# Sparse attention in a two-block transformer kernel: compressed keys stored ahead of the first key set and scored with it, their softmax done per head, retained values transposed one unit sooner

## The chip, the cores and the metric

The kernel runs on one core of one Trainium2 chip. The metric is the device time of one execution in microseconds (us); less is better. The core's engines each run their own instruction stream and meet at semaphores: TensorE (PE, with PEld for its weight loads), VectorE (DVE), ScalarE (ACT), GpSimd (POOL) and SyncE (SP, which only issues the weight DMAs here).

## The reference, cut to what matters

Two transformer blocks on 512 tokens of width 1024. The change lies in the second block, in its sparse attention (`_nsa`), with 16 heads of width 64 in 2 key groups:

```
s_c = einsum('bghqd,bgnd->bghqn', qc, kc) * scale          # 31 compressed keys (windows of 32 tokens)
p_c = _masked_softmax(s_c, cmp_end[None, :] <= t[:, None])
o_c = einsum('bghqn,bgnd->bghqd', p_c, vc)
...                                                        # selected blocks: here all 8 blocks of 64 tokens are taken
o_s = softmax(q . k_slc, causal) . v_slc
o_w = softmax(q . k_win, causal) . v_win
return gc[..., 0:1] * o_c + gc[..., 1:2] * o_s + gc[..., 2:3] * o_w
```

With 512 tokens the selection takes every block and the window covers every key, so each head has two causal attentions over 512 keys (`m` = 0 selected, `m` = 1 window) and a third over the 31 compressed keys, padded to 32. Beside it the block has a retention branch, whose values `rv` are projected, centred and transposed in the same stretch of the program.

## The kernel before

**Units and steps.** `sparse_attention` runs 32 units U. Four of them make a group i = U // 4, which is a pair of heads; the place u = U % 4 in it is called a step here, and stands for (head j, key set m) = (0,0), (0,1), (1,0), (1,1). Each engine has a part that loops over the 32 units in a fixed, hand-written order; semaphores with absolute counts order the parts against each other.

**What TensorE does in a step** (`pe_part`): it transposes the probabilities of U by key blocks kb (`turn(U, 0)`, `turn(U, 1)`: 7 transposes, `bank<-ident,nprob`), does the first half of a projection of 1024 x 128 weights (`fill`, 12 matmuls of 512 columns, three for each of 4 tiles, since every product is made of high and low parts), transposes the rest (`turn(U, 2)`, `turn(U, 3)`: 3 transposes), does the second half of `fill` (12 matmuls), then scores unit U + 2 (`score`, 4 query blocks qb of (qb + 1) x 128 keys, each with two matmuls), and last multiplies by the values (`values`, 8 matmuls). The transposes kb = 2 and 3 go into the banks of kb = 0 and 1, and so wait until VectorE has read those (`lo`).

**What is done for the compressed keys**, once in a group: `compressed_scores(i + 1)` in step 2, 16 matmuls of 32 columns for both heads, into bank 7; `compressed_shift(i + 1)` on VectorE at the start of step 3 (mask, row maximum, subtraction: 3 instructions of 256 elements); `compressed_exps` on ScalarE in step 3; `compressed_scale(i)` on VectorE in step 0; then `compressed_turn(i, 0)` at the end of step 0 and `compressed_turn(i, 1)` in step 1 (4 transposes each, `bank<-ident,cpad`), each copied out of bank 7 as a high part by ScalarE (`cpt_hi`) and a low part by VectorE (`cpt_lo`), and used by `compressed_values` (`bank<-cpt_hi,vcs`) in steps 0 and 2. `retained_values(i)` (`bank<-centre,rv_t`) uses the same bank 7 in step 2.

**What VectorE does in a step**, in order (`dve_part`): `biased(U + 1)`, which adds the mask to the scores of the next unit and takes the row maxima (L2382, four, with a small instruction behind, L2387); the low parts of the transposes kb = 0 and 1 (`npt_lo`, L2422); extra work of the step; the low parts kb = 2 and 3; `scaled(U + 1)` (three small instructions and four of L2405); and the low part of a weight chunk (`w_lo`, L162). ScalarE in a step makes the high parts (`npt_hi`, L2280), the exponentials (L2251) and the high part of the weight chunk.

**Where a score goes.** Query blocks are scored in the order 0, 2, 1, 3: blocks 0 and 2 in bank 0, block 1 in bank 1, block 3 in bank 2. `score` of a unit waits for the `biased` of the unit before it on the same banks.

Of the kernel before, what the change touches and what calls it, by code (L numbers as in the profile page):

```python
# [79 lines left out]
def build_program(nc, stream, xt, cols, tables, rows, decays, pos, w2, out):  # L80
    top = ExitStack()
    with top:
# [1552 lines left out]
        kc_a = sb("kc_a", [P, 32], F32R, A0 + 11 * K)  # L1635
        kc_b = sb("kc_b", [P, 32], F32R, A0 + 11 * K + 256)
# [18 lines left out]
        nk_a = sb("nk_a", [P, 2, S], F32R, A0 + 64 * K)  # L1655
        nk_b = sb("nk_b", [P, 2, S], F32R, A0 + 68 * K)
        nvs = sb("nvs", [P, TB, 2, P], F32R, A0 + 72 * K)
# [369 lines left out]
        def sparse_attention(start):  # L2027
# [6 lines left out]
                                              "c_scored", "c_dve", "c_exp", "c_turned", "c_hi", "c_lo", "zero",  # L2034
# [20 lines left out]

            def score(pe, U):
                j, m = units[U % 4]
                if U % 16 < 2:
                    pe.wait_ge(s["k_lo"], k_ready(U // 16, m))
                if U % 4 == 0:  # L2060
                    pe.wait_ge(s["q_done"], 2 * (U // 4 + 1))
                for n, qb in enumerate(SCORE_ORDER):
                    at_least(pe, s["biased"], 4 * (U - 1) + max(n, 1) + 1, z["biased"])
                    at = slice(qb * P, (qb + 1) * P)
                    mm2(score_bank(qb), nq[:, j, at], nk_a[:, m, 0:(qb + 1) * P], nk_b[:, m, 0:(qb + 1) * P]
                        ).then_inc(s["scored"], 1)

            def compressed_bank(i):
                return banks[7] if i else banks[3]

            def compressed_scores(pe, i):
                pe.wait_ge(s["q_done"], 2 * i + 2)
                pe.wait_ge(s["k_lo"], k_ready(i // 4, "kc"))
                at_least(pe, s["rv_lo"], i)
                for j in range(2):
                    for qb in range(TB):
                        at = slice(qb * P, (qb + 1) * P)
                        last = mm2(compressed_bank(i)[:, (TB * j + qb) * 32:(TB * j + qb + 1) * 32], nq[:, j, at],
                                   kc_a[:], kc_b[:])
                    last.then_inc(s["c_scored"], 1)  # L2080

            def first_scores(pe):
                pe.wait_ge(q["out"], 12)
                compressed_scores(pe, 0)
                score(pe, 0)

            def pe_part(pe):
# [54 lines left out]
                for U in range(UNITS):  # L2142
# [8 lines left out]
                    if U == 0:  # L2151
                        pe.wait_ge(s["c_dve"], 1)
# [20 lines left out]
            def high_k(g):  # L2173
                for m in range(2):
                    k = nqk[:, g + 8 + 2 * m, :]
                    nc.scalar.activation(nk_a[lower, m, :], k[lower], ACT.Copy).then_inc(s["k_hi"], 1)
                    nc.scalar.activation(nk_b[upper, m, :], k[upper], ACT.Copy).then_inc(s["k_hi"], 1)
# [36 lines left out]
            def low_k(pool, g, base):  # L2214
                for m in range(2):
                    k = nqk[:, g + 8 + 2 * m, :]
                    for n, (r, to, hi) in enumerate(((lower, nk_b, nk_a), (upper, nk_a, nk_b))):
                        pool.wait_ge(s["k_hi"], base + 2 * m + n + 1)
                        nc.gpsimd.tensor_tensor(to[r, m, :], k[r], hi[r, m, :], ALU.subtract).then_inc(s["k_lo"], 1)
# [22 lines left out]
            def compressed_exps(act, i):  # L2242
                act.wait_ge(s["c_dve"], 10 * i + 3)
                nc.scalar.activation(csc[:], csc[:], ACT.Exp, scale=0.125).then_inc(s["c_exp"], 1)
# [9 lines left out]
            def first_exps(act):  # L2254
                exps(act, 0, range(TB))
                compressed_exps(act, 0)

            def act_part(act):

                def stage_k(g):  # L2260
                    at_least(act, s["scored"], 64 * g, z["scored"])
                    at_least(act, s["c_scored"], 8 * g)
# [51 lines left out]
                for U in range(UNITS):  # L2314
# [8 lines left out]
                    if u == 1:  # L2323
                        compressed_high(i, 1)
                    if u == 2:
# [8 lines left out]
                    if u == 0:  # L2334
                        compressed_high(i, 0)
                    ahead(high_part, act, fn, U)
                    if u == 1 and i < 7:
                        stage_q(i + 1)
                        if i == 3:
                            stage_k(1)  # L2340
                    if u == 3 and i < 7:
                        compressed_exps(act, i + 1)
# [13 lines left out]
            add = cmp_add[:].rearrange("p (o t) n -> p o t n", o=1).to_broadcast([P, 2, TB, 32])  # L2356
            keep = cmp_keep[:].rearrange("p (o t) n -> p o t n", o=1).to_broadcast([P, 2, TB, 32])
            over = [t.rearrange("p (h t o) -> p h t o", h=2, o=1).to_broadcast([P, 2, TB, 32])
                    for t in (c_top, c_inverse)]

            def step(dve, i, instruction, count, wait=True):

                instruction.then_inc(s["c_dve"], 1)
                if wait:
                    dve.wait_ge(s["c_dve"], 10 * i + count)

            def compressed_shift(dve, i):
                dve.wait_ge(s["c_scored"], 2 * i + 2)
                step(dve, i, nc.vector.tensor_tensor(
                    csc[:], compressed_bank(i)[:, 0:256].rearrange("p (h t n) -> p h t n", h=2, t=TB), add, ALU.add), 1)  # L2370
                step(dve, i, nc.vector.tensor_reduce(c_top.rearrange("p (h t) -> p h t", h=2), csc[:], AX.X, ALU.max), 2)
                step(dve, i, nc.vector.tensor_tensor(csc[:], csc[:], over[0], ALU.subtract), 3, False)

            def biased(dve, U):
                for place_of, qb in enumerate(SCORE_ORDER):
# [6 lines left out]
                    nc.vector.tensor_tensor_reduce(nprob[:, U % 2, scores_rows(qb)], score_bank(qb),  # L2382
# [24 lines left out]
            def first_shift(dve):  # L2407
                compressed_shift(dve, 0)
# [6 lines left out]
            def dve_part(dve):  # L2415
# [26 lines left out]
                def compressed_scale(i):  # L2442
                    dve.wait_ge(s["c_exp"], i + 1)
                    step(dve, i, nc.vector.tensor_tensor(csc[:], csc[:], keep, ALU.mult), 4)
                    step(dve, i, nc.vector.tensor_reduce(c_total.rearrange("p (h t) -> p h t", h=2), csc[:], AX.X, ALU.add), 5)
                    step(dve, i, nc.vector.tensor_scalar(c_total, c_total, 1e-20, None, ALU.max), 6)
                    step(dve, i, nc.vector.reciprocal(c_total, c_total), 7)
                    step(dve, i, nc.vector.tensor_tensor(
                        c_inverse.rearrange("p (h t) -> p h t", h=2), c_total.rearrange("p (h t) -> p h t", h=2),
                        gates[:, :, i * 6:i * 6 + 6].rearrange("p t (h c) -> p h t c", c=3)[:, :, :, 0], ALU.mult), 8)  # L2450
                    for j in range(2):

                        diagonal = cpad[:, j, :].rearrange("p (t w) -> p t w", w=P + 32)[:, :, 0:32]
                        step(dve, i, nc.vector.tensor_tensor(diagonal, csc[:, j, :, :], over[1][:, j, :, :], ALU.mult), 9 + j,
                             False)
# [9 lines left out]
                for U in range(UNITS):  # L2465
                    i, u = U // 4, U % 4
                    if u == 3 and i < 7:
                        compressed_shift(dve, i + 1)
# [3 lines left out]
                    if u == 0:  # L2472
                        compressed_scale(i)
                        if i:
                            joined(i - 1, 1)
                    if u == 1:
                        compressed_low(i, 1)
                    if u == 2:
                        retained_low(i)
                    lows(U, (2, 3))  # L2480
                    if u == 0:
                        compressed_low(i, 0)
                    if u == 2:
                        joined(i, 0)
# [604 lines left out]
```

## Time and profile before

| | |
|---|---|
| median of 3 runs | 2149.85 us (2149.74 to 2151.31) |
| the profiled execution | 2148.9 us, of which the traced span is 2147.2 us |
| PE busy | 2107.7 us (98%) |
| DVE busy | 1328.0 us (62%) |
| ACT busy | 1006.7 us (47%) |
| POOL busy | 690.0 us (32%) |
| mean granted TensorE clock | 0.993 |
| stretch of the 32 units | about 1229 to 1556 us from the span's start |

Times in the trace are microseconds from the start of the span; L2382 is line 2382 of the kernel. A timeline row of TensorE shows its start and a modelled end, so a matmul's price in a dense stream is read from the start of one row to the start of the next. In a row of VectorE or ScalarE the second figure is the instruction's length, or with `xN` behind it that of N in a row.

### The profile page before, as it was taken

The page shows a single profiled execution, that of the slowest core. Times are in us where ns is not written, and L with a number is a line of the kernel's source. Part 1 is how long each engine was busy: PE and PEld are TensorE (multiplying, and loading weights), DVE is VectorE, ACT ScalarE, POOL GpSimd, SP SyncE. Part 2 cuts the span into 40 slices and gives each one's busy share as a digit, 9 for nine tenths or more (in the row PEclk, how much of TensorE's full clock was granted, in tenths as well). Part 3 has the DMA queues.
Part 4 walks back from the last instruction along what each step waited for, and adds up shares of the span by engine and source line. Part 5 has one row for each costly group of instructions (what it writes and reads, how often), then busy time and mean ns, then how long its engine had stood idle before and what let it go on. Part 6 is the DMA issues. An engine that isn't in the chain of part 4 may idle for free.

```text
span 2147.2 us, 31300 instructions
## 1 busy us (share of the span) xinstructions
PE 2107.7 (98%) x10824; PEld 1784.2 (83%) x10824; DVE 1328.0 (62%) x2185; ACT 1006.7 (47%) x1770; POOL 690.0 (32%) x515
## 2 busy tenths in 40 slices
PE   8999999999999999999999999999999999999997
PEld 6887888889988888898887788888877888889886
DVE  5467774467672276765268788788768336676524
ACT  4345564533442263344234467676656325334322
POOL 2011345323233262443325601211165415132331
PEclk9999999999999999999999999999999999999999
DMA  5212235243433333443334322222264533434331
GB/s 171 79 50 69 84 121 183 94 134 140 163 115 108 95 117 117 147 161 103 98 102 147 118 69 70 84 74 77 86 210 140 185 98 118 136 131 166 105 95 62
DMA packets 73423, 248.15 MB, mean 116 GB/s; under 512 B 8080, under 2 KB 8336, under 8 KB 72944
## 3 DMA queue, kind: packets, MB, share of 16 engines
q1 hardware_dynamic: 51120, 182.08, 26.8%
q0 software_dynamic: 10496, 37.56, 5.1%
q10 hardware_dynamic: 11712, 27.27, 3.5%
q8 instruction: 57, 0.93, 0.2%
q14 instruction: 38, 0.31, 0.1%
HBM read 227.48 MB, written 18.87 MB: 115 GB/s over the span
## 4 chain that ended last, share of the span: by engine, by line
PE 85%; DVE 8%; ACT 2%; issue 2%; POOL 2%; DMA 1%; DVEq 0%; SPq 0%; ACTq 0%; POOLq 0%
PE bank L188 25%; PE bank L189 24%; PE bank L190 24%; PE bank L194 3%; PE bank L195 3%; POOL hid L709 2%; PE bank L2095 2%; DVE w_lo L162 1%; DVE gn_r L2697 1%; DVE xn_lo L587 1%; PE bank L883 1%; PE bank L2756 1%; PE bank L2758 1%; DMA w_raw<-stream 1%; DVE blk L1929 1%
## 5 line engine op out<-in xcount | busy, mean ns | idle before, releaser
L162 DVE TENSOR_TENSOR w_lo<-w_raw,w_hi 128x1024 fp32r<-128x1024 f32 x337 | 449.9, 1339 | 424.7 <-ACT w_hi L157 422.1
L188 PE MATMUL bank<-xn_hi,w_hi 128*128 128x512 f32 (+1 forms) x1432 | 555.0, 388 | 7.0 <-DVE w_lo L162 6.1
L157 ACT ACTIVATE w_hi<-w_raw 128x1024 fp32r<-128x1024 f32 x337 | 354.6, 1054 | 409.5 <-PE bank L190 248.2
L189 PE MATMUL bank<-xn_lo,w_hi 128*128 128x512 f32 (+1 forms) x1432 | 540.6, 378 | 0.0
L190 PE MATMUL bank<-xn_hi,w_lo 128*128 128x512 f32 (+1 forms) x1432 | 540.0, 377 | 0.0
L188 PEld LDWEIGHTS bank<-xn_hi,w_hi 128*128 128x128 f32 x1432 | 271.7, 190 | 58.3 <-DVE w_lo L162 7.2
L190 PEld LDWEIGHTS bank<-xn_hi,w_lo 128*128 128x128 f32 x1432 | 270.7, 189 | 50.2
L189 PEld LDWEIGHTS bank<-xn_lo,w_hi 128*128 128x128 f32 x1432 | 271.6, 190 | 45.4 <-issue 2.6
L188 PE MATMUL bank<-down_hi,w_hi 128*128 128x512 f32 x528 | 205.9, 390 | 0.0
L190 PE MATMUL bank<-down_hi,w_lo 128*128 128x512 f32 x528 | 205.6, 389 | 0.0
L189 PE MATMUL bank<-down_lo,w_hi 128*128 128x512 f32 x528 | 205.6, 389 | 0.0
L763 POOL TENSOR_TENSOR down_lo<-h,down_hi 128x512 fp32r<-128x512 f32 x66 | 111.9, 1700 | 252.9 <-ACT down_hi L543 252.9
L189 PEld LDWEIGHTS bank<-down_lo,w_hi 128*128 128x128 f32 x528 | 99.1, 188 | 20.9 <-issue 0.2
L188 PEld LDWEIGHTS bank<-down_hi,w_hi 128*128 128x128 f32 x528 | 99.2, 188 | 20.6 <-POOL down_lo L763 0.2
L190 PEld LDWEIGHTS bank<-down_hi,w_lo 128*128 128x128 f32 x528 | 99.1, 188 | 20.6
L509 ACT ACTIVATE snaps<-bank 128x256 f32<-128x256 f32 x96 | 36.8, 384 | 164.9 <-PE bank L190 164.8
L498 ACT ACTIVATE silu<-silu 128x512 f32<-128x512 f32 x66 | 41.6, 631 | 150.9 <-DVE silu L596 85.7
L714 POOL DMA_DIRECT2D s_raw<-stream x48 | 26.5, 553 | 231.7 <-DVE s_lo L609 231.2
L2211 POOL TENSOR_TENSOR q_low<-nqk,nq 64x512 f32<-64x512 f32 x16 | 21.4, 1336 | 213.2 <-ACT nq L2195 212.5
L601 DVE TENSOR_TENSOR h<-silu,h 128x512 f32 (+1 forms) x66 | 84.3, 1277 | 4.4
L190 PE MATMUL bank<-t_hi,s_lo 128*128 128x256 f32 x288 | 81.6, 283 | 0.0
L189 PE MATMUL bank<-t_lo,s_hi 128*128 128x256 f32 x288 | 81.5, 283 | 0.0
(451 smaller groups left out, 4261.8 us busy)
## 6 DMA issues: line engine op xcount, KB each, us to landing
w_raw<-stream SPq DMA_DIRECT2D x337, 512.0 KB, 3.6
s_raw<-stream POOLq DMA_DIRECT2D x48, 512.0 KB, 6.3
spill_g<-gate_out ACTq DMA_DIRECT2D x16, 256.0 KB, 2.0
m_more<-spill_g POOLq DMA_DIRECT2D x3, 1024.0 KB, 12.8
x<-xt SPq DMA_DIRECT2D x4, 512.0 KB, 7.7
x<-xt ACTq DMA_DIRECT2D x1, 2048.0 KB, 9.9
spill_x<-x ACTq DMA_DIRECT2D x1, 2048.0 KB, 6.4
spill_ga<-ga_out ACTq DMA_DIRECT2D x8, 256.0 KB, 2.0
```

Source lines behind the costliest of these rows:

```text
L157: nc.scalar.activation(w_hi[:, slot, :], w_raw[:, slot % 2, :], ACT.Copy).then_inc(split_hi, 1)
L162: nc.vector.tensor_tensor(w_lo[:, slot, :], w_raw[:, slot % 2, :], w_hi[:, slot, :], ALU.subtract).then_inc(split_lo, 1)
L188: nc.tensor.matmul(to, a_hi, b_hi, start=start, stop=False, skip_group_check=True)
L189: nc.tensor.matmul(to, a_hi, b_lo, start=False, stop=False, skip_group_check=True)
L190: return nc.tensor.matmul(to, a_lo, b_hi, start=False, stop=stop, skip_group_check=True)
L194: nc.tensor.matmul(to, both, first, start=start, stop=False, skip_group_check=True)
L195: return nc.tensor.matmul(to, both, second, start=False, stop=stop, skip_group_check=True)
L498: nc.scalar.activation(silu[t][:], silu[t][:], ACT.Silu).then_inc(s["silu"], 1)
L601: nc.vector.tensor_tensor(to, silu[t][:], to, ALU.mult).then_inc(s["product"], 1)
L709: nc.gpsimd.tensor_tensor(total_sq, squares[:, 0, :] if k == 1 else total_sq, squares[:, k % 4, :], ALU.add).then_inc(m["added"], 1)
L763: nc.gpsimd.tensor_tensor(down_lo[:, j % 4, :], h[:, bass.ds(k * S, S)], down_hi[:, j % 4, :], ALU.subtract).then_inc(s["lo"], 1)
L2095: last = nc.tensor.transpose(banks[4 + kb % 2][:, (qb - kb) * P:(qb - kb + 1) * P], nprob[:, U % 2, OFF[qb] + kb * P:OFF[qb] + (kb + 1) * ...
```

## The change

What it does:

- The high and low compressed keys `kc_a`, `kc_b` become the first 32 columns of `nk_a`, `nk_b`, directly in front of key set m = 0.
- `compressed_scores` is gone. In a `score` with m = 0, the matmuls of query blocks 0, 1 and 2 take 32 columns more (160, 288, 416 in place of 128, 256, 384), and block 3, which fills a bank by itself, gets a separate pair of 32 columns, written into bank 1. The query blocks are scored in the order 0, 1, 2, 3 (0 and 1 in bank 0, 2 in bank 1, 3 in bank 2).
- The softmax of the compressed keys is done per head: `compressed_shift(i, 1)` at the start of VectorE's step 1 and `compressed_shift(i + 1, 0)` at the start of its step 3, each 5 instructions; `compressed_exps` in steps 1 and 3; `compressed_scale(i, 0)` in step 0 and `compressed_scale(i, 1)` in step 2, each 6 instructions on 128 elements or fewer.
- `compressed_turn(i, 1)` moves from step 1 to the end of step 2 (its `cpt_hi` and `cpt_lo` with it), and `retained_values(i)` from step 2 to step 1 (with `rv_hi_out` and `rv_lo_out`).

```diff
-        kc_a = sb("kc_a", [P, 32], F32R, A0 + 11 * K)
-        kc_b = sb("kc_b", [P, 32], F32R, A0 + 11 * K + 256)
...
-        nk_a = sb("nk_a", [P, 2, S], F32R, A0 + 64 * K)
-        nk_b = sb("nk_b", [P, 2, S], F32R, A0 + 68 * K)
+        nk_a = sb("nk_a", [P, NC + 2 * S], F32R, A0 + 64 * K)
+        nk_b = sb("nk_b", [P, NC + 2 * S], F32R, A0 + 68 * K + 4 * NC)
+        kc_a, kc_b = nk_a[:, 0:NC], nk_b[:, 0:NC]
...
+            NORDER = range(TB)
+            AT_C = (banks[0][:, 0:NC], banks[0][:, NC + P:2 * NC + P], banks[1][:, 0:NC], banks[1][:, NC + 3 * P:2 * NC + 3 * P])
...
-                for n, qb in enumerate(SCORE_ORDER):
+                for n, qb in enumerate(NORDER):
                     at_least(pe, s["biased"], 4 * (U - 1) + max(n, 1) + 1, z["biased"])
...
+                    if m == 0 and qb < TB - 1:
+                        last = mm2(rows_with_windows(qb), nq[:, j, at], nk_a[:, 0:NC + width], nk_b[:, 0:NC + width])
+                    else:
+                        last = mm2(rows_bank(qb), nq[:, j, at], keys(nk_a, m, width=width), keys(nk_b, m, width=width))
+                    if m == 0 and qb == TB - 2:
+                        last = mm2(AT_C[TB - 1], nq[:, j, (TB - 1) * P:S], kc_a, kc_b)
+                    last.then_inc(s["scored"], 1)
...
                 def compressed_turn(i, j):
-                    if j == 0:
-                        pe.wait_ge(s["c_dve"], 10 * i + 10)
+                    pe.wait_ge(s["c_dve"], 11 * (2 * i + j + 1))
+                    at_least(pe, s["rv_lo"], i + j)
...
                 def retained_values(i):
                     pe.wait_ge(s["cleared"], 4 * i + 1)
-                    pe.wait_ge(s["c_lo"], 2 * i + 2)
+                    pe.wait_ge(s["c_lo"], 2 * i + 1)
...
                     if u == 1:
-                        compressed_turn(i, 1)
-                    if u == 2:
                         retained_values(i)
...
-                    if u == 0:
-                        compressed_turn(i, 0)
-                    if u == 2 and i < 7:
-                        compressed_scores(pe, i + 1)
+                    if u % 2 == 0:
+                        compressed_turn(i, u // 2)
...
+            def compressed_shift(dve, i, j):
+                dve.wait_ge(s["scored"], 4 * (4 * i + 2 * j) + 3 + z["scored"])
+                near = banks[0][:, 0:2 * (NC + P)].rearrange("p (t w) -> p t w", w=NC + P)[:, :, 0:NC]
+                step(dve, i, j, nc.vector.tensor_tensor(csc[:, j, 0:2], near, cmp_add[:, 0:2], ALU.add), 1, False)
+                for qb in (2, 3):
+                    step(dve, i, j, nc.vector.tensor_tensor(csc[:, j, qb], AT_C[qb], cmp_add[:, qb], ALU.add), qb, qb == 3)
+                step(dve, i, j, nc.vector.tensor_reduce(of_head(c_top, j), csc[:, j], AX.X, ALU.max), 4)
+                step(dve, i, j, nc.vector.tensor_tensor(csc[:, j], csc[:, j], over_windows(c_top, j), ALU.subtract), 5, False)
...
                 for U in range(UNITS):
                     i, u = U // 4, U % 4
+                    if u == 1:
+                        compressed_shift(dve, i, 1)
                     if u == 3 and i < 7:
-                        compressed_shift(dve, i + 1)
+                        compressed_shift(dve, i + 1, 0)
                     if U + 1 < UNITS:
                         biased(dve, U + 1)
                     lows(U, (0, 1))
```

**The order on VectorE, from the end of step 0 into step 1** (L162 is the last instruction of step 0; the ISA rows are `biased`, `npt_lo` the low parts that `turn(U, 2)` and `turn(U, 3)` wait for). Before:

```order
L162 TENSOR_TENSOR w_lo<-w_raw,w_hi 128x1024
L2382 ISA nprob,small<-bank,bias_tri 128x128
L2382 ISA small 128x1
L2382 ISA nprob,small<-bank,bias_tri 128x384
L2382 ISA small 128x1
L2382 ISA nprob,small<-bank,bias_tri 128x256
L2382 ISA small 128x1
L2382 ISA nprob,small<-bank,bias_tri 128x512
L2382 ISA small 128x1
L2387 TENSOR_SCALAR small<-small 128x4
L2422 TENSOR_TENSOR npt_lo<-bank,npt_hi 128x512
L2422 TENSOR_TENSOR npt_lo<-bank,npt_hi 128x384
```

The same place of the changed kernel, up to the first instructions of `biased`:

```order
L162 TENSOR_TENSOR w_lo<-w_raw,w_hi 128x1024
L2367 TENSOR_TENSOR csc<-bank,cmp_add 128x64
L2369 TENSOR_TENSOR csc<-bank,cmp_add 128x32 x2
L2370 TENSOR_REDUCE small<-csc 128x4
L2371 TENSOR_TENSOR csc<-csc,small 128x128
L2381 ISA nprob,small<-bank,bias_tri 128x128
L2381 ISA small 128x1
L2381 ISA nprob,small<-bank,bias_tri 128x256
```

Five instructions now stand between the weight chunk and `biased`; the rest of `biased`, its small instruction and the two `npt_lo` follow as before. Between steps 2 and 3 the same five stand, where three on 256 elements stood.

**The order on TensorE at the end of step 2** (the first row is the last matmul of `fill`; `kc`, 16 matmuls in all, are `compressed_scores`; `nk` is `score`; `cpt` is `compressed_values`). Before, with 13 more `kc` rows in the gap:

```order
L190 MATMUL bank<-xn_hi,w_lo 128x512
L194 MATMUL bank<-kc_a,nq 128x32
L195 MATMUL bank<-kc_b,nq 128x32
...
L195 MATMUL bank<-kc_b,nq 128x32
L194 MATMUL bank<-nk_a,nq 128x128
L195 MATMUL bank<-nk_b,nq 128x128
L194 MATMUL bank<-nk_a,nq 128x384
L195 MATMUL bank<-nk_b,nq 128x384
```

The same place of the changed kernel:

```order
L190 MATMUL bank<-xn_hi,w_lo 128x512
L2114 MATMUL bank<-ident,cpad 128x128 x4
L194 MATMUL bank<-nk_a,nq 128x160
L195 MATMUL bank<-nk_b,nq 128x160
L194 MATMUL bank<-nk_a,nq 128x288
L195 MATMUL bank<-nk_b,nq 128x288
L194 MATMUL bank<-nk_a,nq 128x416
L195 MATMUL bank<-nk_b,nq 128x416
L194 MATMUL bank<-nk_a,nq 128x32
L195 MATMUL bank<-nk_b,nq 128x32
L194 MATMUL bank<-nk_a,nq 128x512
L195 MATMUL bank<-nk_b,nq 128x512
```

The 16 narrow matmuls are gone, and the four transposes of `cpad` have come in their place; behind the scores `cpt` follows as before, now with its input made just in front of it. The end of step 0 reads the same as this in the changed kernel.

## Rows read from the trace of the kernel before

**Rows 1.** The page: the span, and the engines' busy time.

```profile
span 2147.2 us, 31300 instructions
PE 2107.7 (98%) x10824; PEld 1784.2 (83%) x10824; DVE 1328.0 (62%) x2185; ACT 1006.7 (47%) x1770; POOL 690.0 (32%) x515
```

**Rows 2.** Busy time by stretch, a group's length; start:end, length, then engines.

```profile
1312.00:1353.00 41.00, 40.87 (x236) 35.46 (x236) 32.80 (x100) 28.31 (x67) 5.15 (x4) 1.00 0.25 78
```

**Rows 3.** Timeline, TensorE, step 2 to the next step 2; start, us.

```profile
1298.71 0.18 PE L194 MATMUL bank<-kc_a,nq 128*128 128x32 f32 x1
...
1300.41 0.31 PE L194 MATMUL bank<-nk_a,nq 128*128 128x128 f32 x1
...
1307.25 0.48 PE L188 MATMUL bank<-xn_hi,w_hi 128*128 128x512 f32 x1
...
1310.48 0.34 PE L195 MATMUL bank<-nk_b,nq 128*128 128x384 f32 x1
1310.66 0.28 PE L194 MATMUL bank<-nk_a,nq 128*128 128x256 f32 x1
1310.78 0.28 PE L195 MATMUL bank<-nk_b,nq 128*128 128x256 f32 x1
...
1319.21 0.60 PE L2111 MATMUL bank<-ident,cpad 128*128 128x128 f32 x4
...
1321.22 0.50 PE L194 MATMUL bank<-cpt_hi,vcs 128*128 128x512 f32 x1
...
1327.22 0.48 PE L188 MATMUL bank<-xn_hi,w_hi 128*128 128x512 f32 x1
...
1340.07 0.18 PE L194 MATMUL bank<-kc_a,nq 128*128 128x32 f32 x1
```

**Rows 4.** Timeline, VectorE, the same stretch: steps 3, 0 and 1.

```profile
1301.72 0.42 DVE L2369 TENSOR_TENSOR csc<-bank,cmp_add 128x256 f32<-128x256 f32 x1
1302.17 0.42 DVE L2371 TENSOR_REDUCE small<-csc 128x8 f32<-128x256 f32 x1
1302.63 0.42 DVE L2372 TENSOR_TENSOR csc<-csc,small 128x256 f32<-128x256 f32 x1
1302.97 0.28 DVE L2382 CUSTOM_DVE_ANT_0 nprob<-bank,bias_tri 128x128 f32<-128x128 f32 x1
...
1304.81 1.15 DVE L2422 TENSOR_TENSOR npt_lo<-bank,npt_hi 128x512 fp32r<-128x512 f32 x2
...
1320.48 0.69 DVE L2434 TENSOR_TENSOR cpt_lo<-bank,cpt_hi 128x512 fp32r<-128x512 f32 x1 [1.82 <-ACT cpt_hi L2286]
...
1325.86 1.15 DVE L2422 TENSOR_TENSOR npt_lo<-bank,npt_hi 128x512 fp32r<-128x512 f32 x2
```

**Rows 5.** Groups by line and shape, VectorE, 1292.14 to 1333.5; mean ns.

```profile
L2422 DVE TENSOR_TENSOR npt_lo<-bank,npt_hi 128x128 fp32r<-128x128 f32 x4 | 1.1, 281 | 0.0
```

**Rows 6.** Timelines, TensorE and VectorE, into the first unit.

```profile
1217.38 0.25 PE L194 MATMUL bank<-kc_a,nq 128*128 128x32 f32 x1
...
1233.10 0.79 PE L2095 MATMUL bank<-ident,nprob 128*128 128x128 f32 x3 [0.92 <-DVE npt_lo L2422]
...
1219.34 0.42 DVE L2369 TENSOR_TENSOR csc<-bank,cmp_add 128x256 f32<-128x256 f32 x1 [0.90 <-PE bank L195]
...
1220.90 0.28 DVE L2382 CUSTOM_DVE_ANT_0 nprob<-bank,bias_tri 128x128 f32<-128x128 f32 x1
```

**Rows 7.** Timeline, TensorE, group 3 (new keys are staged); its first and last row.

```profile
1360.57 0.60 PE L2111 MATMUL bank<-ident,cpad 128*128 128x128 f32 x4
...
1382.95 0.28 PE L194 MATMUL bank<-kc_a,nq 128*128 128x32 f32 x1 [0.71 <-ACT nq L2202]
...
1405.14 0.60 PE L2111 MATMUL bank<-ident,cpad 128*128 128x128 f32 x4
```

**Rows 8.** Busy time by stretch, TensorE alone, group 3; then its granted clock.

```profile
1384.70:1388.15 3.45, 3.45 (x12) 0.51 0.63 233
```

**Rows 9.** Timeline, TensorE, unit 30, where its second `fill` half ends.

```profile
1550.07 0.39 PE L194 MATMUL bank<-cpt_hi,vcs 128*128 128x512 f32 x1
```

More of the change, by code:

```diff
@@ L2061, in score @@
                     pe.wait_ge(s["q_done"], 2 * (U // 4 + 1))
-                for n, qb in enumerate(SCORE_ORDER):
+                for n, qb in enumerate(NORDER):
                     at_least(pe, s["biased"], 4 * (U - 1) + max(n, 1) + 1, z["biased"])
[L2064 to L2080, printed above, removed]
+                    at, width = slice(qb * P, (qb + 1) * P), (qb + 1) * P
+                    if m == 0 and qb < TB - 1:
[5 more added lines that the diff above has]
+                    last.then_inc(s["scored"], 1)
             def first_scores(pe):
                 pe.wait_ge(q["out"], 12)
-                compressed_scores(pe, 0)
                 score(pe, 0)
@@ L2218, in low_k @@
                         pool.wait_ge(s["k_hi"], base + 2 * m + n + 1)
[L2219 removed]
+                        nc.gpsimd.tensor_tensor(keys(to, m, r), k[r], keys(hi, m, r), ALU.subtract).then_inc(s["k_lo"], 1)
                         pool.wait_ge(s["k_lo"], base + 2 * m + n + 1)
@@ L2354, in act_part, with of_head @@
                 retain[0](act)
[L2356 to L2361, printed above, removed]
+            def of_head(row, j):
+                return row[:, TB * j:TB * j + TB]
@@ L2363, in step, with over_windows @@
+            def over_windows(row, j):
+                return of_head(row, j).rearrange("p (t o) -> p t o", o=1).to_broadcast([P, TB, NC])
+            def step(dve, i, j, instruction, count, wait=True):
                 instruction.then_inc(s["c_dve"], 1)
                 if wait:
[L2365 to L2372, printed above, removed]
+                    dve.wait_ge(s["c_dve"], 11 * (2 * i + j) + count)
@@ L2374, in biased @@
             def biased(dve, U):
-                for place_of, qb in enumerate(SCORE_ORDER):
+                for place_of, qb in enumerate(NORDER):
                     dve.wait_ge(s["scored"], 4 * U + max(place_of, 1) + 1 + z["scored"])
@@ L2381, in biased @@
                     width = (qb + 1) * P
-                    nc.vector.tensor_tensor_reduce(nprob[:, U % 2, scores_rows(qb)], score_bank(qb),
+                    nc.vector.tensor_tensor_reduce(nprob[:, U % 2, scores_rows(qb)], rows_bank(qb),
                                                    bias_tri[:, S - width:S], 1.0, -3.0e38, ALU.add, ALU.max,
@@ L2439, in retained_low, with compressed_scale @@
                     nc.vector.tensor_tensor(rv_lo_out[:], banks[7][:], rv_hi_out[:], ALU.subtract).then_inc(s["rv_lo"], 1)
[L2442 to L2455, printed above, removed]
+                def compressed_scale(i, j):
+                    dve.wait_ge(s["c_exp"], 2 * i + j + 1)
+                    total_c, inverse_c = of_head(c_total, j), of_head(c_inverse, j)
+                    step(dve, i, j, nc.vector.tensor_tensor(csc[:, j], csc[:, j], cmp_keep[:], ALU.mult), 6)
+                    step(dve, i, j, nc.vector.tensor_reduce(total_c, csc[:, j], AX.X, ALU.add), 7)
+                    step(dve, i, j, nc.vector.tensor_scalar(total_c, total_c, 1e-20, None, ALU.max), 8)
+                    step(dve, i, j, nc.vector.reciprocal(total_c, total_c), 9)
+                    step(dve, i, j, nc.vector.tensor_tensor(inverse_c, total_c, gates[:, :, i * 6 + 3 * j], ALU.mult), 10)
+                    diagonal = cpad[:, j, :].rearrange("p (t w) -> p t w", w=P + 32)[:, :, 0:32]
+                    step(dve, i, j, nc.vector.tensor_tensor(diagonal, csc[:, j], over_windows(c_inverse, j), ALU.mult), 11,
+                         False)
                 def rotate(i):
@@ L2471, in dve_part @@
                     lows(U, (0, 1))
[L2472 to L2475, printed above, removed]
+                    if u % 2 == 0:
+                        compressed_scale(i, u // 2)
+                    if u == 0 and i:
+                        joined(i - 1, 1)
+                    if u == 2:
+                        joined(i, 0)
                     if u == 1:
-                        compressed_low(i, 1)
-                    if u == 2:
                         retained_low(i)
                     lows(U, (2, 3))
[L2481 to L2484, printed above, removed]
+                    if u % 2 == 0:
+                        compressed_low(i, u // 2)
                     if U + 1 < UNITS:
```

39 lines of the change are left out of this document (22 added, 17 removed).

## Prediction

> **What bounds the kernel now.** I read the page first: TensorE is busy for 98% of the span and VectorE for 62% [rows 1], so in general only TensorE's work counts. The change lies in the 32 units, so I then read busy time by stretch: in the 41 us of a group TensorE has 40.87 us of work and VectorE 32.80 [rows 2]. TensorE is dense there. What matters next is how far VectorE's results arrive ahead of TensorE's need, and that is in the timelines. A group is 41.36 us long (1298.71 to 1340.07, [rows 3]). I cut it at the ends of `fill` in step 0 and step 2, where the changed kernel has a `compressed_turn` both times: the first half, from step 0 to step 2, takes 1340.07 - 1319.21 = 20.86 us, the second 1319.21 - 1298.71 = 20.50 us [rows 3].
>
> Now VectorE. In step 1 it ends `npt_lo` for kb = 0 and 1 at 1325.86 + 1.15 = 1327.01 [rows 4], and TensorE, whose transposes kb = 2 and 3 wait for them, begins the second half of `fill` at 1327.22 [rows 3], 0.21 us later, without having been idle. There is no slack at this place. In step 3 the same instructions end at 1304.81 + 1.15 = 1305.96 [rows 4] and TensorE begins that half at 1307.25 [rows 3]: about 1.1 us of slack. The zero in step 1 comes from what stands ahead of it: `compressed_turn(i, 0)` at 1319.21, its `cpt_hi`, `cpt_lo` at 1320.48 (VectorE had waited 1.82 us for it), `scaled`, `w_lo`, `biased`, `npt_lo`. From the transposes of `cpad` to the end of `npt_lo` this chain is 1327.01 - 1319.21 = 7.80 us [rows 3, 4].
>
> **The change, part by part.**
>
> TensorE's work. Removed: 16 matmuls of 32 columns, 1300.41 - 1298.71 = 1.70 us a group, 0.11 us each [rows 3]. Added in each of a group's two scores with m = 0: the separate pair, 2 x 0.11 = 0.22, and the wider matmuls. A matmul of 384 columns takes 0.18 us and one of 256 takes 0.12 (1310.48, 1310.66, 1310.78, [rows 3]), so 32 columns cost 0.015; four of them 0.06. Block 0 grows from 128 to 160 columns, and since 256 columns cost hardly more than the 0.11 of 32, this is free. Together 0.28 a score, 0.56 a group. Net work: -1.14 us a group, -9.1 us over 8 groups. `compressed_turn(i, 1)` and `retained_values` only change places.
>
> VectorE's shift. Before: 3 instructions, 1302.97 - 1301.72 = 1.25 us, once a group, in step 3 where there is slack [rows 4]. After: five, in steps 1 and 3. An instruction of 256 elements takes 0.42 us and one of 128 takes 0.28 [rows 4, 5], so 64 take about 0.21 and 32 about 0.18. Two of the five are followed by a wait for the result and one more by a wait behind the third; a dependent instruction starts 0.03 after the end of the one before (1302.17 + 0.42 to 1302.63), a free one 0.08 before it (1302.63 + 0.42 to 1302.97) [rows 4]. That gives 0.13 + 0.10 + 0.21 + 0.31 + 0.20 = 0.95 to 1.0 us; I take 0.99. Bounds: half of the 1.25, 0.63, if only elements cost; and 1.3, if each of the five costs its whole length and a gap.
>
> The Trainium skill, VectorE: DVE Perf Modes, section "The DRAIN you can't avoid", says that chaining instructions without a semaphore saves nothing, since the next one waits for the pipe to empty. By that the five would cost 1.13 to 1.2 us and the sum below would rise by about 2.5 us, which makes the change slower by the bound used below. Here the row disagrees: an instruction of 0.42 us is followed by the next after 0.34 [rows 4].
>
> The new chain. In the changed kernel `compressed_turn` stands at the end of step 0 and of step 2, and the shift stands in steps 1 and 3. Both halves so have the same chain: `cpad` transposes, `cpt_hi`, `cpt_lo`, `scaled`, `w_lo`, shift, `biased`, `npt_lo` kb = 0 and 1, transposes kb = 2 and 3. It takes 7.80 + 0.99 = 8.79 us, and `fill` goes on 0.21 later, 9.00 us behind the `cpad` transposes. From there to the end of the next step's `fill` TensorE has what it had from 1307.25 to 1319.21, 11.96 us [rows 3], if nothing else is late. A half is 20.96 us: +0.10 on the first half and +0.46 on the second, +0.56 a group. So the 1.14 us of work saved turn into a wait of TensorE in front of the transposes kb = 2 and 3, about 1.5 us in step 3 and 0.6 in step 1 (where the 8 matmuls of `retained_values` fill part of it).
>
> Queued behind the shift on VectorE are `biased` and with it the small instruction that ScalarE's exponentials wait for, then the low parts. ScalarE has room: it waits again and again in these steps. The per-head `compressed_scale` costs less in step 0 and comes new in step 2, where it lies ahead of VectorE's wait for `cpt_hi` (1.82 us in step 0, [rows 4]); I cost it at nothing. If that cover were gone, at most its some 1.5 us, once a group, would come in part.
>
> The start. The first shift began at 1219.34, after a wait of 0.90 for the 16 matmuls which began at 1217.38, and `biased` at 1220.90 [rows 6]. Now three pieces of the first score, 8 matmuls, are enough: 1.05 us and the end of the last, about 1218.64, and the shift takes 0.99 and not 1.56. `biased` starts at 1219.63, 1.27 us sooner; TensorE then waited 0.92 us for this chain at 1233.10 [rows 6], so the gain is whole: -1.27.
>
> The end. In unit 30 nothing is scored, and `compressed_values` follows `fill` at once (1550.07, [rows 9]). Now `compressed_turn(7, 1)` comes between, and the values wait for its low part: 1321.22 - 1319.21 = 2.01 [rows 3], plus 0.11 for the weight load that starts late: +2.12.
>
> Group 3. Staging the second set of keys holds ScalarE up, and the group takes 1405.14 - 1360.57 = 44.57 [rows 7], 3.21 more than others. In it TensorE waits 0.71 us for the query copies in front of the narrow matmuls [rows 7], and then runs at a granted clock of 0.51, the level of 1.2 GHz, for 3.45 us [rows 8], which costs half of that, 1.7. In the changed kernel the late low parts would hold TensorE earlier, in front of the transposes, and four transposes come ahead of the wait for the queries; the row of narrow matmuls is gone. I take an excess of 2.1 there (between 0.8, the rest of the 3.21, and all of it), -1.1.
>
> Sum: 8 x 0.10 + 7 x 0.46 (the last group has no second half) = 4.0; start -1.27; end +2.12; group 3 -1.1; together +3.75. The profiled execution of 2148.9 us becomes 2152.6. The median before is 0.95 above that execution, so I say **2153.6 us**.
>
> **The rivals.** A measurement of this kernel can tell about 0.2% from no change, 4.3 us.
>
> (a) The chain, as above: +3.75. For it: zero slack in step 1. The shift's bounds move it by -0.36 and +0.31 for each of 15 halves, -5.4 and +4.7; near the low end TensorE's own work would take over in the first half.
>
> (b) TensorE's work decides: the low parts of `npt_lo` turn out to be in time, and the 1.14 us a group are kept. Then -9.1, -1.3 at the start and +2.1 at the end, about 2141.5. It would need 1.5 us less in the chain, more than the shift costs. Against it stands the 1327.01 beside 1327.22.
>
> (c) The clock. The new waits, 15 of 0.6 to 1.5 us, bring the granted clock down as in group 3. Each fall costs some 1.7 us where TensorE is dense. For it: there it fell behind a wait of only 0.71. Against it: then 16 narrow matmuls followed, and the clock had stayed up in the other groups with the same 16; now full matmuls stand on both sides. Five falls are +8.5, 2162; from the second fall on the result is slower by the bound.
>
> (d) The page's drain rule, +2.5 more, 2156.1: slower.
>
> (e) The shift or the staging is cheaper than I think, near the low bounds: 2149 or so.
>
> **How the numbers follow.** (a) 0.66, of which 0.48 within the bound and 0.18 above it, since 2153.6 lies only 0.5 below the bound of 2154.15; (b) 0.08, all faster; (c) 0.10 and (d) 0.08, all slower; (e) 0.08, of which 0.02 faster. So faster 0.10, within 0.54, slower 0.36. The likeliest case alone spans 2150 to 2157. The range that holds 8 in 10 takes in most of (d) and (e) and the first falls of (c), and leaves out (b): 2147.5 to 2158.5.
>
> **What the changed kernel's profile would show.** TensorE busy about 9 us less, and idle some 13 us more in the 32 units, in front of the transposes `bank<-ident,nprob`, with VectorE `npt_lo` as releaser, more in step 3 than in step 1. A group of 41.9 us, both halves equal. The five shift instructions in 0.99 us. A wait of some 1.5 us before `compressed_values` in unit 30. A clock row of 1.00 through the units. The prediction is wrong if the halves differ, if the idle time has another releaser (`cpt_lo`, or ScalarE's query copies), or if the clock falls again and again.

## Result and profile after

The changed kernel takes **2155.49 us** (median of 20 runs, 2152.73 to 2160.55), the kernel before in the same session 2150.85 (20 runs, 2147.83 to 2155.46). The ratio is 1.0024, 95% interval 1.0017 to 1.0030: slower by 4.6 us, a small slowdown, but one that the interval tells from no change. The forecast was 2153.6 us, with 2147.5 to 2158.5 as the range. Two of the ten runs of e8 below, 2493.71 and 2973.85 us at a mean granted clock of 0.78 and 0.65, are slow ones, and its time is the median of the other eight.

The page of the changed kernel, first its span and busy times, as in [rows 1]:

```profile
span 2155.1 us, 31210 instructions
...
PE 2107.1 (98%) x10728; PEld 1772.6 (82%) x10728; DVE 1348.5 (63%) x2281; ACT 1008.7 (47%) x1778; POOL 690.8 (32%) x515
```

96 matmuls are gone, VectorE has 96 instructions more and is busy for 20 us more. The sum of TensorE hardly moved, though, and must not be read as "no work saved": the ends of matmuls are modelled, and the first block, ahead of the units, ran at other clock rows in this execution. The stretch of [rows 2] is the better place; columns are start:end, length, busy time, granted clock, DMA share, GB/s:

```profile
1312.00:1353.00 41.00, 40.08 (x223) 1.00 0.24 78
```

In it TensorE is busy for 0.79 us less than before (40.87). That did not make the kernel faster, and the timeline of TensorE, step 2 to the next step 2, shows why. It answers to [rows 3]:

```profile
1301.91 0.60 PE L2114 MATMUL bank<-ident,cpad 128*128 128x128 f32 x4
...
1309.04 0.39 PE L190 MATMUL bank<-xn_hi,w_lo 128*128 128x512 f32 x1
1310.29 0.79 PE L2098 MATMUL bank<-ident,nprob 128*128 128x128 f32 x3 [0.86 <-DVE npt_lo L2421]
1310.84 0.48 PE L188 MATMUL bank<-xn_hi,w_hi 128*128 128x512 f32 x1
...
1322.80 0.60 PE L2114 MATMUL bank<-ident,cpad 128*128 128x128 f32 x4
...
1331.17 0.79 PE L2098 MATMUL bank<-ident,nprob 128*128 128x128 f32 x3
...
1343.69 0.60 PE L2114 MATMUL bank<-ident,cpad 128*128 128x128 f32 x4
```

A half is 20.89 us twice (before 20.86 and 20.50), a group 41.78 (before 41.36). In step 3 TensorE stops for `npt_lo`, a wait that was not there. VectorE in the same half, step 3, as in [rows 4]:

```profile
1303.18 0.69 DVE L2433 TENSOR_TENSOR cpt_lo<-bank,cpt_hi 128x512 fp32r<-128x512 f32 x1 [0.78 <-ACT cpt_hi L2282]
...
1306.72 0.22 DVE L2367 TENSOR_TENSOR csc<-bank,cmp_add 128x64 f32<-128x64 f32 x1
1306.86 0.28 DVE L2369 TENSOR_TENSOR csc<-bank,cmp_add 128x32 f32<-128x32 f32 x2
1307.17 0.29 DVE L2370 TENSOR_REDUCE small<-csc 128x4 f32<-128x128 f32 x1
1307.49 0.29 DVE L2371 TENSOR_TENSOR csc<-csc,small 128x128 f32<-128x128 f32 x1
1307.70 0.28 DVE L2381 CUSTOM_DVE_ANT_0 nprob<-bank,bias_tri 128x128 f32<-128x128 f32 x1
...
1309.55 1.15 DVE L2421 TENSOR_TENSOR npt_lo<-bank,npt_hi 128x512 fp32r<-128x512 f32 x2
```

From the `cpad` transposes at 1301.91 to the end of `npt_lo`, 1309.55 + 1.15 = 1310.70, are 8.79 us, in which the shift takes 1307.70 - 1306.72 = 0.98. TensorE begins the second half of `fill` at 1310.84, 0.14 later, and needs 1322.80 - 1310.84 = 11.96 from there. 8.79 + 0.14 + 11.96 = 20.89.

The waits between 1225 and 1570 us (engine, tile and line, releaser: total us, times, longest). PEld is TensorE's weight load, which overlaps the matmuls, so the two do not add up:

```profile
PE bank L2098 <- DVE npt_lo L2421: 8.5, 9, 1.3
...
PE bank L194 <- DVE cpt_lo L2433: 1.4, 1, 1.4
PE bank L2114 <- DVE cpad L2450: 0.4, 1, 0.4
...
PEld bank L2098 <- DVE npt_lo L2421: 20.0, 34, 1.7
```

In the kernel before the waits for `npt_lo` were 1.1 us of matmuls and 2.5 us of weight loads.

**Where the 4.6 us come from.** I cut both traces at the row `bank<-small,pre` (L1803), which stands just ahead of the scores of the first unit, at each `cpad` transpose in step 0, and at `compressed_values` in unit 30. Before, that is 1216.93 to 1550.07, 333.14 us; after, 1219.78 to 1557.58, 337.80 us: **+4.66**. The piece to the first `cpad` in step 0 is -0.21, six ordinary groups are +2.78, group 3 is +0.04, the end +2.05. The spans differ by 7.9 us; 2.85 of it lies ahead of the units, where the code is the same and the clock rows of the two executions differ. The medians (4.64) agree with the units' part. Cut at the first score row itself (1217.38 and 1220.14) the difference is 4.75.

### The profile page after: what moved, and what is told of

The parts are those of the page before. It is cut to its first block, busy times and chain, and to the rows that moved or that the text cites. A ratio compares the mean times of both kernels' runs of the same rounds, so it can differ in the third digit from the quotient of the medians.

```text
span 2155.1 us, 31210 instructions
## 1 busy us (share of the span) xinstructions
PE 2107.1 (98%) x10728; PEld 1772.6 (82%) x10728; DVE 1348.5 (63%) x2281; ACT 1008.7 (47%) x1778; POOL 690.8 (32%) x515
## 4 chain that ended last, share of the span: by engine, by line
PE 83%; DVE 9%; POOL 3%; issue 2%; ACT 2%; DMA 1%; DVEq 0%; SPq 0%; POOLq 0%; ACTq 0%
PE bank L188 25%; PE bank L190 24%; PE bank L189 24%; PE bank L195 2%; PE bank L194 2%; POOL hid L709 2%; PE bank L2098 2%; DVE w_lo L162 1%; DMA w_raw<-stream 1%; DVE xn_lo L587 1%; PE bank L883 1%; DMA m_more<-spill_g 1%; PE bank L1109 1%; DVE blk L1929 1%; POOL hid L1442 1%
## 5 line engine op out<-in xcount | busy, mean ns | idle before, releaser
L162 DVE TENSOR_TENSOR w_lo<-w_raw,w_hi 128x1024 fp32r<-128x1024 f32 x337 | 450.2, 1339 | 422.9 <-ACT w_hi L157 420.2
L2248 ACT ACTIVATE nprob<-nprob,small 128x128 f32<-128x128 f32 (+3 forms) x128 | 70.7, 553 | 33.2 <-DVE small L2386 32.8
```

The lines of the kernel that those rows point to most:

```text
L162: nc.vector.tensor_tensor(w_lo[:, slot, :], w_raw[:, slot % 2, :], w_hi[:, slot, :], ALU.subtract).then_inc(split_lo, 1)
L2248: nc.scalar.activation(at, at, ACT.Exp, bias=neg_top[:, n:n + 1], scale=0.125, accum_out=total[:, n:n + 1]).then_inc(s["exp"], 1)
```

## Experiments

Theory A, the forecast's own: in each half the chain through VectorE decides, TensorE's own work lies some way below it. Theory B: TensorE's own work decides, or one fixed slack, and the 4.66 us come from elsewhere. All kernels are the changed one with one edit. "Units" is the same cut as above, in the profiled execution; "halves" are the times between the `cpad` transposes of ordinary groups.

| kernel | ratio to before (95%) | units, us | halves, us | group 3 |
|---|---|---|---|---|
| changed kernel | 1.0024 (1.0017 to 1.0030) | 337.80 | 20.89 + 20.89 | 44.61 |
| e1, shift later | 0.9972 (0.9962 to 0.9983) | 327.19 | 20.48 + 19.92 | 43.16 |
| e2, turn sooner | 0.9985 (0.9976 to 0.9994) | 329.35 | 20.43 + 20.26 | 44.00 |
| e3, both | 0.9964 (0.9952 to 0.9976) | 324.08 | 20.41 + 19.53 | 43.01 |
| e4, longer shift | 1.0114 (1.0095 to 1.0133) | 357.83 | 21.84 + 21.81 | 47.97 |
| e5, more TensorE work | 1.0019 (1.0010 to 1.0028) | 338.14 | 20.88 + 20.88 | 44.63 |
| e6, GpSimd later | 1.0025 (1.0014 to 1.0036) | 338.47 | 20.90 + 20.91 | 44.90 |
| e7, e3 and e6 | 0.9960 (0.9946 to 0.9974) | 323.28 | 20.36 + 19.46 | 43.35 |
| e8, e3 and e5 | 0.9994 (0.9984 to 1.0004) | 330.10 | 20.86 + 19.97 | 43.63 |

**e1: the shift behind the low parts.** The same work on every engine, but VectorE does `biased` and the `npt_lo` of kb = 0 and 1 first (and TensorE's next scores wait for the shift to have read the banks):

```diff
+                if m == 1:
+                    pe.wait_ge(s["c_dve"], 11 * (U // 2) + 3)
                 for n, qb in enumerate(NORDER):
...
                 for U in range(UNITS):
                     i, u = U // 4, U % 4
-                    if u == 1:
-                        compressed_shift(dve, i, 1)
-                    if u == 3 and i < 7:
-                        compressed_shift(dve, i + 1, 0)
                     if U + 1 < UNITS:
                         biased(dve, U + 1)
                     lows(U, (0, 1))
+                    if u == 1:
+                        compressed_shift(dve, i, 1)
+                    if u == 3 and i < 7:
+                        compressed_shift(dve, i + 1, 0)
```

> The changed kernel with one edit: VectorE does compressed_shift in steps 1 and 3 behind the low parts of kb = 0 and 1 and not ahead of biased. The same five instructions stay, and TensorE's work is untouched. (A wait is added on TensorE ahead of the scores with m = 1, for the shift's three reads, which by then have long been done.) Theory A, the shift is on the chain that holds TensorE's transposes kb = 2 and 3: the 0.97 us leave the chain, which falls below TensorE's own path; the group goes from 41.8 to about 40.4 us, the 32 units lose some 11 us, and the kernel ends near 2144.5, below the kernel before by 0.25 to 0.35%. The idle time in front of bank<-ident,nprob <- npt_lo falls from 28 us to below 8. Rival B, TensorE loses its time to the added narrow matmuls and to compressed_turn standing at the end of step 2: no change, 2155. Rival C, any work added to VectorE in these steps costs its length wherever it stands: no change either.

Measured: 2146.05 us, 11 us under the changed kernel by the ratios (0.9972 against 1.0024). The experiments ran in two sessions, each with the kernel before in it, so between sessions ratios are compared, not medians. In the timeline of VectorE the pair stands in the other order:

```profile
1307.36 1.15 DVE L2423 TENSOR_TENSOR npt_lo<-bank,npt_hi 128x512 fp32r<-128x512 f32 x2
1308.42 0.21 DVE L2369 TENSOR_TENSOR csc<-bank,cmp_add 128x64 f32<-128x64 f32 x1
```

And of the waits for `npt_lo` these are left:

```profile
PE bank L2100 <- DVE npt_lo L2423: 2.4, 3, 1.3
...
PEld bank L2100 <- DVE npt_lo L2423: 7.9, 18, 1.7
```

That is 10.3 us where the changed kernel had 28.5 (both sums count matmuls and weight loads); I had expected less than 8. A group came down to 20.48 + 19.92 = 40.40 us. The place of the shift, not its being there, is what cost.

**e2: the second `compressed_turn` one weight block sooner.** This shortens the same chain from its other end: the transposes of `cpad` stand ahead of the last block of `fill`.

```diff
-                    fill(slot, range(4, KT)).then_inc(used, 1)
                     if u % 2 == 0:
+                        fill(slot, range(4, 7))
                         compressed_turn(i, u // 2)
+                        fill(slot, range(7, KT)).then_inc(used, 1)
+                    else:
+                        fill(slot, range(4, KT)).then_inc(used, 1)
```

> The changed kernel with one edit: in steps 0 and 2 compressed_turn stands ahead of the last of the eight tiles of fill, three matmuls or 0.69 us sooner; the shift stays where the change put it. Theory A, the chain runs from the transposes of cpad over cpt_hi, cpt_lo, scaled, w_lo, shift, biased to npt_lo: starting it 0.69 us sooner shortens each half by up to that, to about 20.3 us; the group becomes 40.6, the end gains 0.5 more, together about -10 us, near 2145.5. If cpad is late in step 2, TensorE waits there and the gain is smaller, some -6. Rival B, the chain does not start at cpad but at the exponentials of the next unit or at w_lo: no change. Rival C, TensorE's work decides: no change.

Measured: 2147.68 us, ratio 0.9985, 8.4 us under the changed kernel; a group of 40.69. A new wait comes with it, for `compressed_scale`, seven times in the weight loads:

```profile
PEld bank L2098 <- DVE npt_lo L2424: 11.6, 20, 1.7
...
PEld bank L2114 <- DVE cpad L2453: 3.5, 7, 1.4
```

**e3: both orders.** The diffs of e1 and e2 together.

> Both orders together: the shift behind the low parts of npt_lo, and the second compressed_turn ahead of the last block of fill. Theory A (the changed kernel's halves are held by the chain, and TensorE's own work lies below it): each order alone left waits for npt_lo, 7.9 and 11.6 us in TensorE's weight loads; together they should go nearly to nothing, and a group should come down to TensorE's own work, 39.6 to 40.0 us, below 40.40 of the late shift alone. That is 13 to 17 us under the changed kernel, near 2140. Theory B (a single slack of fixed size, which either order gives): no gain beyond the late shift alone, 2146 within 2 us, a group of 40.4.

Measured: 2141.29 us, ratio 0.9964, a group of 39.94. The waits:

```profile
PE bank L2100 <- DVE npt_lo L2426: 2.2, 2, 1.3
...
PEld bank L2100 <- DVE npt_lo L2426: 4.0, 6, 1.7
...
PEld bank L2116 <- DVE cpad L2455: 3.5, 7, 1.4
```

Theory A gives this; a single fixed slack, used up by e1, does not: 3 us more came off the units. (The intervals of the two ratios overlap; the difference rests on the second halves, 19.53 against 19.92 us.) And 2141.3 is close to the 2141.5 that my rival (b) gave for the case that the chain is in time. That agreement is partly luck. Against the kernel before, six ordinary groups are -8.50 us here, group 3 -1.56, the start -0.52 and the end +1.52, where (b) had -9.1 for all groups, -1.3 and +2.1. An ordinary group gained 1.42 us, not 1.14.

**e4: a longer shift.** Two additions of 256 elements from one constant table into a scratch tile stand ahead of the shift, 15 times:

```diff
             def compressed_shift(dve, i, j):
                 dve.wait_ge(s["scored"], 4 * (4 * i + 2 * j) + 3 + z["scored"])
+                if i + j:
+                    for n in range(2):
+                        nc.vector.tensor_tensor(spare[:], bias_tri[:, 0:256], bias_tri[:, 256:512], ALU.add).then_inc(spared, 1)
+                        dve.wait_ge(spared, 2 * (2 * i + j - 1) + n + 1)
```

> The changed kernel with two more VectorE instructions of 128x256 into a spare tile at the head of each compressed_shift but the first (15 times), about 0.80 us each time. Theory A, the shift is on the chain in both halves of a group and nothing gives way: +0.80 x 15 = +12 us, near 2167.5, the group at 43.4. Rival B, the chain has slack in one half: +5 to +6. Rival C, TensorE's work decides: 0.

Measured: 2174.54 us, 19 us over the changed kernel. VectorE's timeline gives the length of the pair, 1310.27 - 1309.36 = 0.91:

```profile
1309.36 0.88 DVE L2371 TENSOR_TENSOR spare<-bias_tri 128x256 f32<-128x256 f32 x2
1310.27 0.22 DVE L2374 TENSOR_TENSOR csc<-bank,cmp_add 128x64 f32<-128x64 f32 x1
```

Eleven of 15 halves grow by 0.9 and no more: the chain hands on all of it. The other four grow by some 1.5 us more, and in just these the granted clock fell. Busy time of TensorE in the four stretches:

```profile
1269.37:1272.78 3.41, 3.41 (x10) 0.50 0.00 0
1358.12:1361.53 3.41, 3.41 (x10) 0.50 0.02 5
1405.91:1409.32 3.41, 3.39 (x10) 0.50 0.00 0
1539.03:1542.44 3.41, 3.41 (x9) 0.50 0.00 0
```

15 x 0.92 + 4 x 1.57 = 20.1; the units grew by 20.03. I had expected 12, from a pair of 0.80 us and no fall of the clock. So the sum holds, and my rival (c) is a real mechanism, which the changed kernel stayed clear of: its longest wait for `npt_lo` in the weight loads is 1.7 us, here 2.5. The length of the wait alone does not decide, though. The matmuls' waits ahead of the four falls were 1.77, 1.76, 2.08 and 1.77 us, and three others of 1.77 to 1.78 (at 1313.84, 1450.64 and 1494.29) had no fall behind them.

**e5: more work on TensorE.** The pair of 32 columns of query block 3 is done three times instead of once, 0.11 us a matmul, 0.45 us in each of 16 scores:

```diff
                     if m == 0 and qb == TB - 2:
+                        for _ in range(2):
+                            mm2(AT_C[TB - 1], nq[:, j, (TB - 1) * P:S], kc_a, kc_b)
                         last = mm2(AT_C[TB - 1], nq[:, j, (TB - 1) * P:S], kc_a, kc_b)
```

> The changed kernel with the separate pair of 32 columns done three times in each score with m = 0: 4 more matmuls, 0.45 us more TensorE work, 16 times, 7 us in all. Theory A, TensorE waits later in the same half for npt_lo, longer than 0.45 us, so the added work is taken out of that wait: 0 to +1 us. Rival B, TensorE's work decides: +7 us, near 2162.5.

Measured: 2155.27 us, no change, and halves of 20.88. The 7.2 us of added work went into the waits, which were 8.5 and 20.0 us in the changed kernel:

```profile
PE bank L2100 <- DVE npt_lo L2423: 6.4, 9, 1.3
...
PEld bank L2100 <- DVE npt_lo L2423: 12.5, 18, 1.7
```

**e8: the same added work, on e3.** The diff of e5, on top of e3.

> The two orders together and the 0.45 us of extra TensorE work in each of 16 halves, which the changed kernel took for nothing. Theory A: with the chain out of the way TensorE's own work decides, and the same extra work now costs nearly its length, 16 x 0.45 = 7.2 us over the two orders alone. Theory B (something else than the chain absorbs it, a wait at another place): it costs less than 2 us here too.

Measured: 2148.4 us, 7.1 over e3 by the medians, 6.5 by the ratios (0.9994 against 0.9964) and 6.0 in the units; forecast 7.2. Where the chain is out of the way, the same matmuls cost their length: a group takes 40.82 to 40.85 against 39.94. With e5 this is the plainest of the pairs: one edit, worth nothing in one order of VectorE's and TensorE's queues and 6 to 7 us in the other.

**e6: GpSimd later.** The two rotation instructions wait until the second `compressed_scale` is done:

```diff
                     pool.wait_ge(s["r_swapped"], i + 1)
+                    pool.wait_ge(s["c_dve"], 11 * (2 * i + 2))
                     nc.gpsimd.tensor_tensor(r_swap[:], r_swap[:], ret_s[:], ALU.mult).then_inc(s["r_sines"], 1)
```

> The changed kernel with GpSimd's two instructions on the rotated values held back until compressed_scale(i, 1) is done. Theory: the small VectorE instructions of compressed_scale in step 2 take 0.9 to 1.1 us where they lie beside GpSimd's work and 0.17 to 0.2 elsewhere; moved apart, the one of 0.99 falls to about 0.17. It lies ahead of VectorE's wait for cpt_hi, which has 0.78 us left, so ordinary groups stay at 41.8; the time moves by -1 to 0 us, 2155. Rival: these instructions are long by themselves, or because of TensorE or ScalarE; then they stay at 0.99 in step 2.

Measured: 2154.67 us, ratio 1.0025, nothing. The cause it asked after was found, though. In the changed kernel, step 2, VectorE and GpSimd:

```profile
1341.33 0.99 DVE L2446 TENSOR_SCALAR small<-small 128x4 f32<-128x4 f32 x1
...
1340.99 1.30 POOL L2503 TENSOR_TENSOR r_qk<-r_qk,r_swap 128x512 f32<-128x512 f32 x1 [0.16 <-issue]
```

In e6, the same instruction, ahead of GpSimd's:

```profile
1337.07 0.17 DVE L2446 TENSOR_SCALAR small<-small 128x4 f32<-128x4 f32 x1
...
1338.15 1.30 POOL L2500 TENSOR_TENSOR r_swap<-r_swap,ret_s 128x512 f32<-128x512 f32 x1 [2.72 <-DVE cpad L2450]
```

0.82 us less, and `csc<-csc,cmp_keep` (L2444), two instructions ahead of it, fell from 0.52 to 0.28. The wait for `cpt_hi` behind them grew by the sum, 1.06, from 0.78 to 1.84: hidden, as forecast. In the changed kernel the long instruction ended when GpSimd's did, 1341.33 + 0.99 = 1342.32 beside 1340.99 + 1.30 = 1342.29.

**e7: e3 and e6.** All three diffs.

> The late shift, the sooner second compressed_turn and the GpSimd instructions held back, all three. If compressed_scale in step 2 comes to stand on the path once the second compressed_turn is sooner (TensorE waited there for VectorE's cpad 4.5 us in seven places when that order was tried alone), holding GpSimd back gives 2 to 4 us more than the two orders without it: near 2137. If the small instructions are hidden there, no difference from the two orders alone.

Measured: 2141.45 us, ratio 0.9960. The seven waits for `cpad` are down to one and a group to 39.82, 0.12 less than e3, but the time is that of e3 within the interval. The cheaper version, e3, is the one to keep; it is 0.4% faster than the kernel before.

## Why the forecast was right, and where not

- **The chain (rival a): right, almost to the row.** Forecast 7.80 + 0.99 = 8.79; in the trace 8.79. The time by itself would have fitted rival (d), 2156.1, better; it is the rows that decide for (a). e1 and e2 shorten it from either end and gain, e4 lengthens it and pays in full, e5 and e8 rule out TensorE's own work. Two equal halves, releaser `npt_lo`, as forecast.
- **The shift: 0.98 for 0.99.** The rule of the Trainium skill, VectorE: DVE Perf Modes, section "The DRAIN you can't avoid", would have made it 1.13 to 1.2; the trace does not bear it out here. The same section adds that a next instruction that is not held starts earlier, which the forecast left out, and the trace agrees with that. The second of two unchained instructions (1306.86, 0.28 for both) shows the overlap. Rival (d) is out.
- **An ordinary group: +0.46, forecast +0.56.** `fill` goes on 0.14 behind the chain, not 0.21. Over six groups that is +2.78 for +3.36.
- **The end: +2.05**, forecast 2.01 and the 0.10 of the last first half; the 0.11 for the weight load lies just behind this cut. TensorE waited 1.41 us for `cpt_lo` in unit 30.
- **The start: this term was mis-sized, -0.21 for -1.27.** `biased` starts 3.07 us after the cut, where I had 2.70, and before 3.97. Of the 0.9 gained 0.7 went again, in an instruction that I had not counted, since it had been short:

```profile
1222.19 0.73 DVE L2371 TENSOR_TENSOR csc<-csc,small 128x128 f32<-128x128 f32 x1
...
1224.60 0.90 DVE L2386 TENSOR_SCALAR small<-small 128x4 f32<-128x4 f32 x1
```

  ScalarE's exponentials wait for the second, which took 0.20 in the kernel before at this place. From the start of `biased` to the first `cpad` transpose it is 15.59 us in the kernel before and 16.28 in the changed one, 0.69 more, which is what this instruction gained. GpSimd worked without a gap in both kernels. In the changed one the instruction ended at 1225.50, beside a GpSimd instruction that ended at 1225.46; in the kernel before it fell at the end of one (1222.85 beside 1222.83). No experiment moved GpSimd here, so for the start the cause is only read off, by what e6 showed in step 2.
- **Group 3: mis-sized too, +0.04 for -0.54.** The clock fall went away as forecast (clock 1.00 through the units), but the step "I cost it at nothing", the second `compressed_scale` in step 2, came in here. VectorE, then TensorE:

```profile
1383.09 1.16 DVE L2421 TENSOR_TENSOR npt_lo<-bank,npt_hi 128x512 fp32r<-128x512 f32 x2 [1.81 <-ACT npt_hi L2276]
...
1385.11 0.89 DVE L2446 TENSOR_SCALAR small<-small 128x4 f32<-128x4 f32 x1
1386.03 0.18 DVE L2447 RECIPROCAL small<-small 128x4 f32<-128x4 f32 x1
1386.24 1.12 DVE L2448 TENSOR_TENSOR small<-small,gates 128x4 f32<-128x4 f32 x1
...
1383.84 0.79 PE L2098 MATMUL bank<-ident,nprob 128*128 128x128 f32 x3 [1.25 <-DVE npt_lo L2421]
...
1387.74 0.66 PE L2114 MATMUL bank<-ident,cpad 128*128 128x128 f32 x4 [0.35 <-DVE cpad L2450]
```

  The scaling takes 1387.68 - 1384.16 = 3.5 us, where it takes 1.6 in step 0 and 2.6 in step 2 of an ordinary group; two small instructions are stretched beside GpSimd's key staging, and TensorE waits for `cpad`. How the rest of group 3's 2.8 us of excess divides was not tried.
- **What I expected of the page was half wrong.** "Busy about 9 us less" does not show in the page's sum (-0.6). Over the cut of the units, before, changed and e3:

```profile
1216.93:1550.07 333.14, 330.09 (x1873) 0.99 0.24 74
...
1219.78:1557.58 337.80, 325.53 (x1778) 1.00 0.23 72
...
1217.06:1541.14 324.08, 318.35 (x1778) 1.00 0.25 76
```

  Busy time fell by 4.6 us and idle time grew by 9.2 (3.05 to 12.27), where I had 9 and 13. But e3 has the same matmuls and shows 7.2 us less busy time than the changed kernel, so part of what counts as busy there is not work. The waits were also shorter than forecast: the matmuls' wait for `npt_lo` is 0.86 us in step 3 for "about 1.5", and in step 1 only weight loads wait (0.39 and 0.26) for "0.6".

The errors of the terms are +1.06 (start), +0.58 (group 3), -0.58 (ordinary groups) and -0.06 (end). The total at this cut, +4.66 for the forecast's +3.66 (4.02 for the halves, which the forecast rounded to 4.0), is 1.0 us off; two errors of the same size cancelled, and what is left is the start's. That they cancelled is luck. Of the 1.9 us between 2153.6 and the measured 2155.49, 1.0 is the session, in which the kernel before took 2150.85 and not 2149.85, and 0.9 the change, +4.64 for +3.75. By the forecast's own bound of 4.3 us the change, at +4.64, falls just on the slower side, to which the forecast gave 0.36, and not within it (0.54).

## What to carry to other kernels

When work is taken off the engine that is busy 98% of the time, follow the chain to its next wait before counting the gain: with zero slack there, a microsecond put ahead of it on another engine cancels the saving. Then ask whether the new work must stand ahead of what is waited for: the same instructions behind it, and their input a block sooner, turned 0.24% slower into 0.4% faster. To tell which of two engines decides, add the same small work to it in both orders (e5 and e8) rather than read busy shares.

## What the hardware showed that I had not expected

- VectorE instructions of 4 elements a partition, 0.17 us elsewhere, took 0.9 to 1.1 us in some places beside a GpSimd instruction, and 0.17 again when that was moved (e6). One of 128 elements, the last of the first shift, took 0.73 at the start, 0.29 in the groups, and 0.29 to 0.80 at the start of the experiments. Four kernels whose work is the same from the first score row to the first `cpad` transpose (the changed one, e1, e4, e6) take 18.81 to 19.06 us over it, and that spread is this instruction's, 0.57 to 0.80: from `biased` on all four take 16.27 to 16.29.
- The granted clock fell to 0.50, the level of 1.2 GHz, for 3.41 us four times in e4. The matmuls had waited 1.76 to 2.08 us ahead of the falls, about 0.9 longer than in the changed kernel, in which the clock never fell in the units; but three waits of the same length in e4 had no fall behind them. The kernel before had one fall in the units, in group 3 [rows 8]. A fall cost 1.57 us, a little less than half its length.
